# Down projections as seven half-block products, with their weight and gate sums on POOL and DVE

## The reference

```python
def conv_ffn(h, w_up, conv_w, conv_b, w_down):
    S = h.shape[1]
    u = h @ w_up
    up = jnp.pad(u, ((0, 0), (CONV_W - 1, 0), (0, 0)))
    u = conv_b + sum(conv_w[j] * up[:, j:j + S] for j in range(CONV_W))
    gate, val = jnp.split(u, 2, axis=-1)
    return (jax.nn.silu(gate) * val) @ w_down
```

## Time and profile before

| | us |
|---|---|
| median of 3 runs | 1197.97 (1197.91 to 1198.34) |
| span of the profiled execution | 1195.8 |
| TensorE busy in it | 1189.6 |
| DVE, ACT, POOL busy | 756.1, 561.5, 202.0 |
| first, second down projection | 119.7, 119.7 |

### The profile page before, as it was taken

The page is one execution under the profiler, slowest core; times in us unless marked ns, Lnnn a source line. Parts: engine busy times, 40 slices in busy tenths (PEclk is TensorE's granted clock), DMA queues, the critical chain, the costliest instruction groups (busy, mean ns, idle before and its releaser), DMA issues.

```text
span 1195.8 us, 17325 instructions
## 1 busy us (share of the span) xinstructions
PE 1189.6 (99%) x6082; PEld 974.4 (81%) x6082; DVE 756.1 (63%) x1331; ACT 561.5 (47%) x936; POOL 202.0 (17%) x297
## 2 busy tenths in 40 slices
PE   9999999999999999999999999999999999999998
PEld 7768886778888888888888987988888888888887
DVE  6588967945766566563335998845766566563334
ACT  6554337845433333342225789945443333342321
POOL 0533546820000000000000467720000000000000
PEclk9999999999999999999999999999999999999999
DMA  7522231213332232213232210023332222213232
GB/s 270 185 89 90 71 107 53 73 53 106 110 127 79 105 105 73 102 54 105 90 103 93 88 37 2 2 71 106 107 122 87 105 105 70 105 53 106 88 105 105
DMA packets 26673, 110.84 MB, mean 93 GB/s; under 512 B 2896, under 2 KB 3280, under 8 KB 19456
## 3 DMA queue, kind: packets, MB, share of 16 engines
q1 hardware_dynamic: 26624, 110.21, 27.0%
HBM read 108.06 MB, written 6.33 MB: 96 GB/s over the span
## 4 chain that ended last, share of the span: by engine, by line
PE 97%; ACT 1%; DVE 1%; issue 0%; POOL 0%; DVEq 0%; ACTq 0%; POOLq 0%
PE ps L2164 29%; PE ps L2166 28%; PE ps L2165 28%; PE ps L1931 3%; PE ps L1915 3%; PE ps L1731 1%; PE ps L2130 1%; PE ps L1772 1%; PE ps L1802 1%; PE ps L1899 1%; ACT probs L837 1%; PE ps L1783 0%; PE ps L1739 0%; DVE probs L1308 0%; PE ps L1711 0%
## 5 line engine op out<-in xcount | busy, mean ns | idle before, releaser
L1188 DVE TENSOR_TENSOR w_lo<-raw,w_hi 128x1024 fp32r<-128x1024 f32 (+2 forms) x108 | 179.9, 1665 | 263.0 <-ACT w_hi L747 263.0
L747 ACT ACTIVATE w_hi<-raw 128x1024 fp32r<-128x1024 f32 (+2 forms) x118 | 170.9, 1448 | 222.1 <-PE ps L2166 221.8
L2164 PE MATMUL ps<-h_hi,w_hi 128*128 128x512 f32 x704 | 274.6, 390 | 0.0
L2166 PE MATMUL ps<-h_hi,w_lo 128*128 128x512 f32 x704 | 274.1, 389 | 0.0
L2165 PE MATMUL ps<-h_lo,w_hi 128*128 128x512 f32 x704 | 274.1, 389 | 0.0
L2164 PE MATMUL ps<-a_hi,w_hi 128*128 128x512 f32 x480 | 187.6, 391 | 0.0
L2166 PE MATMUL ps<-a_hi,w_lo 128*128 128x512 f32 x480 | 187.0, 390 | 0.0
L2165 PE MATMUL ps<-a_lo,w_hi 128*128 128x512 f32 x480 | 187.0, 390 | 0.0
L1011 ACT ACTIVATE cv<-u_in,vec 128x512 f32<-128x512 f32 x88 | 71.2, 816 | 182.7 <-DVE u_in L1501 180.6
L2164 PEld LDWEIGHTS ps<-h_hi,w_hi 128*128 128x128 f32 x704 | 132.2, 188 | 28.0 <-issue 0.7
L2165 PEld LDWEIGHTS ps<-h_lo,w_hi 128*128 128x128 f32 x704 | 132.2, 188 | 27.2
(11 more groups left out here) (234 smaller groups left out, 1618.6 us busy)
## 6 DMA issues: line engine op xcount, KB each, us to landing
raw<-in_f_up SPq DMA_DIRECT2D x44, 1024.0 KB, 4.8
raw<-in_f_w_down SPq DMA_DIRECT2D x44, 512.0 KB, 3.3
raw<-in_a_in_wide SPq DMA_DIRECT2D x12, 1024.0 KB, 4.9
bias_tiles<-bias_rows SPq DMA_DIRECT2D x1, 4096.0 KB, 20.3
raw<-in_a_w_out SPq DMA_DIRECT2D x8, 512.0 KB, 3.3
raw<-in_b_w_out SPq DMA_DIRECT2D x7, 512.0 KB, 3.3
xT<-in_xt SPq DMA_DIRECT2D x8, 256.0 KB, 7.0
raw<-in_a_in_wide SPq DMA_DIRECT2D x8, 256.0 KB, 7.1
```

Source lines behind the costliest of these rows:

```text
L747: sc.activation(w_hi[:, s, 0:n], raw[:, s, 0:n], ACT.Copy).then_inc(w_hi_done, 1)
L1188: dve.tensor_tensor(w_lo[:, s, 0:n], raw[:, s, 0:n], w_hi[:, s, 0:n].bitcast(F32), ALU.subtract)\
L2164: pe.matmul(dst, s_hi, m_hi, start=start, stop=False)
L2166: return pe.matmul(dst, s_lo, m_hi, start=False, stop=stop)
```

## The change

Both down projections are computed by Strassen's scheme. A pair of tiles (two blocks of 128 rows of w_down), the two halves of the output features and the two halves of the tokens form a 2 x 2 x 2 block product; seven products of half size replace eight. Each is 4 blocks x 3 matmuls of 256 columns. They accumulate over the 11 pairs, in two phases, because the seven results don't fit with their operands at once: phase one makes M1, M3, M6, M2 for all pairs (units 0 to 10), phase two M4, M5, M7 (units 11 to 21). The weights of every pair are therefore loaded twice (768 KB a unit, in three buffers: raw's two and raw2).

The operands are sums and differences. POOL makes two weight sums of 512 columns per unit (`weight_sums`), DVE the third of a phase-one unit (`g_third` in `seven_lo`). POOL makes three gate sums of 256 columns per pair (`gate_sums`), for all but the last pair in its order ahead of the weight sums; DVE makes two more per pair in phase one (`gate_differences`). ACT rounds, DVE subtracts, as before but in halves of a unit. Between the phases DVE adds M1 and M6 out of PSUM to the residual, ACT copies M3 and M2 to SBUF (`cv`), and DVE adds them from there during phase two. M4, M5 and M7 are added at the end, between the steps that prepare layer two (`into_second_layer`), whose weights are split in eight pieces; their loads are queued on SP behind the units. In layer two `into_output` does the adds alone, and the output goes out in 12 DMAs. Loops over tiles become straight code; the semaphores of the two layers are merged. The core of the diff:

```diff
+SEVEN = {"M1": (0, 0, 2), "M3": (1, 1, 0), "M6": (2, 3, 4), "M2": (3, 2, 6),
+         "M4": (2, 2, 2), "M5": (0, 1, 0), "M7": (1, 0, 4)}
+G_PAIRS = FT // 2
+G_UNITS = 2 * G_PAIRS
+G_USED = 2 * G_UNITS - 3
+G_PARTS = ((("M1", "M3"), ("M6", "M2")), (("M4",), ("M5", "M7")))
...
+SUMMED_IN = {**{i + 2: (i,) for i in range(G_PAIRS - 2)}, 4: (2, 9), 7: (5, 10)}
...
+def w_part(u, p):
+    if first_of_two(u):
+        return slice(D, SLOT) if p else slice(0, D)
+    return slice(0, D) if p else slice(D, D + HD)
+def g_part(u, p):
+    if first_of_two(u):
+        return slice(S, 2 * S) if p else slice(0, S)
+    return slice(0, S) if p else slice(S, S + HS)
...
         with ExitStack() as scope:
+            g_hi1 = sb("g_hi1", [P, 2 * S], F32R, scope)
+            g_lo1 = sb("g_lo1", [P, 2 * S], F32R, scope)
+            raw2 = sb("raw2", [P, SLOT], F32, scope)
...
-                with sp.Fori(0, FT // 2) as i:
-                    for s in range(2):
-                        load(U_DOWN[l] + 2 * i + s, down_v[l][2 * i + s], raw[:, s, 0:D], s)
+                for u in range(G_UNITS):
+                    r, k = u % 3, 2 * pair_of(u)
+                    if u == 2:
+                        sp.wait_ge(f_done, 2 * FT * l + 4 * UP_STEPS)
+                    else:
+                        sp.wait_ge(w_lo_done, U_DOWN[l] + u - (1 if u < 2 else 2))
+                    if first_of_two(u):
+                        sp.dma_start(raws[r][:, HD:HD + D], down_v[l][k]).then_inc(g_raw[r], 16)
+                        sp.dma_start(raws[r][:, HD + D:SLOT], down_v[l][k + 1][:, HD:D]).then_inc(g_raw[r], 16)
+                    else:
+                        sp.dma_start(raws[r][:, 0:HD], down_v[l][k][:, 0:HD]).then_inc(g_raw[r], 16)
+                        sp.dma_start(raws[r][:, HD:HD + D], down_v[l][k + 1]).then_inc(g_raw[r], 16)
...
+            sp.dma_start(raw[:, 1, 0:4 * B_DOWN], b_w_down[1]).then_inc(w_raw[1], 16)
+            sp.wait_ge(w_lo_done, U_B)
+            sp.dma_start(raw[:, 0, :].rearrange("p (a n) -> p a n", a=2)[:, :, 0:2 * B_DOWN],
+                         b_w_down[0].rearrange("p (a n) -> p a n", a=2)).then_inc(w_raw[0], 16)
+            for s in (1, 0):
...
+            def gate_sums(l, i):
+                even, odd = act[:, 2 * i], act[:, 2 * i + 1]
+                if i == 0:
+                    pool.wait_ge(ss_ok, 2 * l + 2)
+                pool.wait_ge(f_act, FT * l + 2 * i + 2)
+                pool.tensor_tensor(g_pair[i][:, 0:HS], even[:, 0:HS], odd[:, HS:S], ALU.add)
+                chain.then_wait(pool.tensor_tensor(g_pair[i][:, HS:S], even[:, HS:S], odd[:, HS:S], ALU.subtract))
+                pool.tensor_tensor(even[:, HS:S], even[:, 0:HS], even[:, HS:S], ALU.add).then_inc(g_pre, 1)
+            def weight_sums(l, u):
+                r = u % 3
+                s0, s1, s2, s3 = (raws[r][:, j * HD:(j + 1) * HD] for j in range(4))
+                pool.wait_ge(g_raw[r], g_landed(l, u))
+                if first_of_two(u):
+                    chain.then_wait(pool.tensor_tensor(s0, s1, s3, ALU.add))
+                    pool.tensor_tensor(s3, s2, s3, ALU.add).then_inc(g_sum, 1)
+                else:
+                    chain.then_wait(pool.tensor_tensor(s0, s0, s1, ALU.add))
+                    pool.tensor_tensor(s1, s1, s2, ALU.subtract).then_inc(g_sum, 1)
+            def sums_of_layer(l):
+                for i in range(G_PAIRS - 1):
+                    gate_sums(l, i)
+                for u in range(4):
+                    weight_sums(l, u)
+                gate_sums(l, G_PAIRS - 1)
+                for u in range(4, G_UNITS):
+                    weight_sums(l, u)
...
+            def seven_hi(l, u, p):
+                s = u % 2
+                sc.wait_ge(g_sum, G_UNITS * l + u + 1)
+                if p and first_of_two(u):
+                    sc.wait_ge(g_third, G_PAIRS * l + u + 1)
+                if u >= 2:
+                    last = 1 if u in (G_PAIRS, G_PAIRS + 1) else p
+                    sc.wait_ge(r_used[1], G_USED * l + 2 * (u - 2) + last + 1)
+                else:
+                    sc.wait_ge(f_done, 2 * FT * l + 4 * UP_STEPS - 2 + 2 * u)
+                at = w_part(u, p)
+                sc.activation(w_hi[:, s, at], raws[u % 3][:, at], ACT.Copy)\
+                    .then_inc(w_hi_done if p else g_hi_first, 1)
+                if first_of_two(u):
+                    sc.wait_ge(g_pre, G_PAIRS * l + pair_of(u) + 1)
+                else:
+                    sc.wait_ge(g_diffed, G_PAIRS * l + pair_of(u) + 1)
+                sc.activation(g_hi[s][:, g_part(u, p)], g_source(u, p), ACT.Copy).then_inc(r_hi[1], 1)
+            def seven_products(l):
+                for u in range(2, G_UNITS):
+                    for p in range(2):
+                        seven_hi(l, u, p)
+                    if u in (G_PAIRS, G_PAIRS + 1):
+                        j = u - G_PAIRS
+                        sc.wait_ge(r_used[1], G_USED * l + 2 * G_PAIRS - 1 + j)
+                        sc.activation(cv[:, 2 * j:2 * j + 2, :].rearrange("p a (b n) -> p (a b) n", n=HS),
+                                      bank_tiles(("M3", "M2")[j], 0, 4), ACT.Copy).then_inc(g_copied, 1)
...
+            def into_second_layer():
+                down_piece_hi(4)
+                down_piece_hi(5)
+                sc.wait_ge(g_done, 3)
+                down_piece_hi(6)
+                features_hi(2, 4, G_MIX + KD)
+                features_hi(2, 5, G_MIX + KD)
+                down_piece_hi(7)
+                features_hi(2, 6, G_MIX + KD)
+                features_hi(2, 7, G_MIX + KD)
+                sc.wait_ge(g_done, 4)
+                down_piece_hi(0)
+                down_piece_hi(1)
+                square_of(2, 4)
+                square_of(2, 5)
+                sc.wait_ge(g_done, 8)
+                features_hi(2, 0, G_MIX + KD)
+                features_hi(2, 1, G_MIX + KD)
...
+                features_hi(2, 3, G_MIX + KD)
+                down_piece_hi(3)
+                for k in (6, 7, 0, 1, 2, 3):
+                    square_of(2, k)
+                table(ACT.Sqrt)
+                for k in range(2):
...
+            def seven_lo(l, u, p):
+                s = u % 2
+                if p:
+                    dve.wait_ge(w_hi_done, U_DOWN[l] + u + 1)
+                else:
+                    dve.wait_ge(g_hi_first, G_UNITS * l + u + 1)
+                if p == 0 and first_of_two(u):
+                    third, taken = raws[u % 3][:, D:D + HD], raws[u % 3][:, HD:D]
+                    dve.wait_ge(g_sum, G_UNITS * l + u + 1)
+                    dve.tensor_tensor(third, third, taken, ALU.subtract).then_inc(g_third, 1)
+                at = w_part(u, p)
+                dve.tensor_tensor(w_lo[:, s, at], raws[u % 3][:, at], w_hi[:, s, at].bitcast(F32), ALU.subtract)\
+                    .then_inc(w_lo_done if p else g_lo_first, 1)
+                dve.wait_ge(r_hi[1], 2 * G_UNITS * l + 2 * u + p + 1)
+                at = g_part(u, p)
+                dve.tensor_tensor(g_lo[s][:, at], g_source(u, p), g_hi[s][:, at].bitcast(F32), ALU.subtract)\
+                    .then_inc(r_lo[1], 1)
+            def gate_differences(l, i):
+                even, odd = act[:, 2 * i], act[:, 2 * i + 1]
+                if i == 0:
+                    dve.wait_ge(f_act, FT * l + FT)
+                chain.then_wait(dve.tensor_tensor(g_diff[:, (i + 8) % G_PAIRS], odd[:, 0:HS], even[:, 0:HS],
+                                                  ALU.subtract))
+                dve.tensor_tensor(odd[:, 0:HS], odd[:, 0:HS], odd[:, HS:S], ALU.add).then_inc(g_diffed, 1)
+            def onto(l, count, c, t, source, op):
+                x = x_quarter(c, t)
+                dve.wait_ge(g_out, 10 * l + count - 1)
+                dve.tensor_tensor(x, x, source, op).then_inc(g_out, 1)
+            def seven_products(l):
+                m3, m2 = (cv[:, 2 * p:2 * p + 2, :].rearrange("p a (b n) -> p (a b) n", n=HS) for p in range(2))
+                for u in range(2, G_UNITS):
+                    seven_lo(l, u, 0)
+                    if u == G_PAIRS:
+                        dve.wait_ge(g_done, 8 * l + 1)
+                        x = x_quarter(1, 1)
+                        dve.tensor_tensor(x, x, bank_tiles("M1", 0, 4), ALU.add).then_inc(g_out, 1)
+                        onto(l, 2, 0, 0, bank_tiles("M1", 0, 4), ALU.add)
+                    seven_lo(l, u, 1)
+                    if u == G_PAIRS:
+                        dve.wait_ge(g_done, 8 * l + 2)
+                        onto(l, 3, 1, 1, bank_tiles("M6", 0, 4), ALU.add)
+                    if u == G_PAIRS + 2:
+                        dve.wait_ge(g_copied, 2 * l + 1)
+                        onto(l, 4, 1, 1, m3, ALU.add)
+                    if u == G_PAIRS + 3:
+                        onto(l, 5, 0, 1, m3, ALU.add)
+                    if u == G_PAIRS + 4:
+                        dve.wait_ge(g_copied, 2 * l + 2)
```

(120 more changed lines are left out.)

252 lines of the change are left out of this document (148 added, 104 removed).

## The result

The changed kernel takes 1251.08 us (median of 4 runs, 1248.67 to 1253.8) against 1197.97: ratio 1.0443 (95% interval 1.0425 to 1.046), 53 us slower. The prediction was 1243.4, its range 1204 to 1264. The profiled execution took 1248.67, the shortest of the four; its span is 1246.8, 51.0 us more than before. The median lies 4.3 us above this span; for the kernel before it was 2.2, and that is the rest of the 53.

What follows compares the result with a forecast made beforehand. TensorE was taken to bound the kernel, then DVE taking turns with POOL: stage 140.9 us against 119.7, 42.4 us more in both layers, plus 2.0 and 1.0, on 1197.97 gives 1243.4 us, range 1204 to 1264.

Steps and rivals of the forecast that it cites:

- What binds: TensorE bounds the old kernel, busy for 99% of the span; after the change DVE's work plus POOL's sets the down stages.
- POOL's turns: Down stages: POOL reading SBUF and DVE with two SBUF inputs exclude each other per instruction; 45.6 + 1.8 us per layer.
- TensorE's part: Down projections: 924 matmuls of 256 columns per layer, 0.12 us apart, 110.9 us, 8.8 us less per layer.
- Rival 3: Down stages: weight loads bind at 256 columns, following at 0.19 us; stage 175.6 us, total 1310; chance 1%.
- The price of a turn: Down stages: a POOL sum beside DVE costs 1.14 us for 512 columns (alone 1.29), 0.60 for 256.
- The ledger: Down stage: DVE 86.1 us plus POOL 45.6 and 1.8 is 133.5; with TensorE's 4.3 and 3.1 for passing work on, 140.9.
- TensorE's part behind the last weights: End of each down stage: 3 x 12 matmuls of M5 and M7 after DVE's last weights, 4.3 us.
- the hand-over: Down stages: a sum must land before ACT copies, ACT before DVE subtracts; 0.14 us for each of 22 units, 3.1 us.
- Rival 4: Down stages: TensorE's pauses lower its clock from 2.4 GHz and matmuls double while it lasts; beyond 1264 us, chance 2%.
- The loads: Down stages: a unit's 768 KB land in about 4.1 us; three buffers give two units or more of lead, 8.6 us; covered.
- The gate sums in the up projection: Up projection: POOL's gate operations for ten pairs, where POOL is empty and DVE has 50.6 us to spare; costed at nothing.
- Seam and end: Into layer two DVE's preparation comes later, 2.0 us with waits; at the very end its adds cost 1.0 more.

Runs made afterwards that it cites:

- The memsets: The changed kernel with POOL's two weight sums per unit replaced by two memsets of 1420 columns that read nothing, sums left out of the result: 1187.09 us.

## Why the prediction was right

- **What binds.** Right: TensorE in the kernel before; then DVE, lengthened by POOL's turns. The memsets, the third sum on POOL and all sums on DVE each go the way of the turns, by 64, 11 and 31 us.
- **TensorE's part.** 924 x 0.12 = 110.9: 111.4 to 111.7 where nothing else binds. Rival 3 is out.
- **The price of a turn, 1.14 us for 512 columns.** Right for a single meeting: POOL ends 1.15 and 1.16 after DVE in the timeline. As a mean it was too high: DVE is busy for 39.6 us (133.4 - 93.8) more than beside the memsets in the first stage, 35.9 in the second, 0.99 and 0.90 for each of 40 sums. In phase one it is 1.2 and 1.1, in phase two 0.8 and 0.7; why it is less there, no run shows.
- **The ledger.** 140.9 was forecast for a stage, measured 143.5 and 142.9. This sum is the mis-sized term, by 2.3 us a layer, and its parts are off by more and partly cancel: the closeness is in part luck. Left out was 5.3 us of DVE's work: the three adds of M1 and M6, "kept apart" because they read PSUM and so take no turns, but DVE makes them in the stage all the same (3.4); the last scaled result (0.6); and the wait between the two gate operations of each pair, 0.12 x 11 (1.3). Too small was TensorE's part behind the last weights, 5.7 for 4.3: it is still busy with M5 of the unit before when they are ready. Too small was the hand-over, 3.1, where DVE is idle for 4.3 and 7.6. Too large were the turns: 137.8 - 4.3 - 86.1 - 5.3 = 42.1 us in the first stage and 38.3 in the second, not 47.4. The memset kernel bears the rest out: there DVE is busy for 93.8 us up to its last weights, and 86.1 + 5.3 and the 1.8 of the last pair's gate sums are 93.2.
- **What the total is off by.** 7.7 us in all: 4.6 from the two stages, 1.0 from the end less 0.2 at the seam, and about 2.1 because the median lies 4.3 us above the profiled span and not 2.2, as the prediction had left it.
- **Not one microsecond per unit.** "TensorE will wait in nearly every unit, about 1 us in each" is wrong in shape: 4.9 us before unit 2 in both layers, 3.5 twice more in the first and 3.0 once in the second, several of 1.0 to 2.5, and none before many a unit.
- **Rival 4, the clock.** The mechanism came, the price didn't. In layer one units 2, 5 and 10 take 8.0, 7.2 and 8.2 us instead of 5.64 and unit 15 loses 1.5, 8.0 us together; in layer two units 2 and 3 take 7.2 each, 3.1 together. The stages differ by 0.5 us. TensorE waits for DVE anyway, and a slow unit mostly uses up that time. This was argued from the trace; no run holds the clock up with the pauses in place.
- **The loads.** They aren't "two units or more" ahead: POOL waits 62 us for them in the first stage. They wait for DVE's remainder three units back, so this follows from the binding and doesn't cause it: with the same loads the memset kernel has one pause, of 0.6 us.
- **The gate sums in the up projection** cost nothing, though the first of each pair lasts 2.7 us instead of 0.74.
- **Seam and end.** Seam 1.8 against 2.0, in part by luck: DVE's work from the last weights to the sum of squares took 21.0 us (671.85 to 692.81) instead of 19.4, with 1.4 us of waiting for ACT in it, but began 5.7 us before TensorE was through instead of 4.3. End 2.0 against 1.0: not DVE's adds, which end 1.1 us after the start of TensorE's last matmul, as before, but the output behind them, 4.4 us instead of 2.4. SP issues eight DMAs of 128 KB from 1241.28 to 1245.05:

```profile
1241.28 1.79 SPq L644 DMA_DIRECT2D out_y<-xT  x4
1243.12 1.93 SPq L647 DMA_DIRECT2D out_y<-xT  x4
```

The prediction never counted the issues of the 12 output DMAs, though the diff shows them.

## What to carry to other kernels

An idle engine is free only if the busy one needn't take turns with it: before giving POOL work that reads SBUF beside DVE's work with two SBUF inputs, add POOL's time to DVE's (here 0.9 to 1.0 us of DVE's time for a sum of 1.29). Sum such a ledger per phase, and put in every operation of the engine that binds, also those that take no turns, and 0.12 us for each wait between dependent ones. What depends on inputs alone can be made by adding DMAs into HBM while the queues are idle, one at a time and away from loads that are about to be needed.
